# Two experts' tokens sorted at once into transposed form, the usual path behind the test, and one key and value chunk in place of two, in a four-layer model on one core

## The reference, cut to what matters

```python
hid = jax.nn.silu(xi @ w1[e]) * (xi @ w3[e])     # w1, w3: 1024 x 512
return hid @ w2[e]                               # w2: 512 x 1024
...
h = modulate(rms_norm(x, norm_ffn[layer]), sh_f, sc_f)      # hn * (1 + scale) + shift
x = x + gt_f[:, None, :] * hier_moe(h, ...)
```

```python
h = rms_norm_2(x, norm_g) @ w_in
q, kv, gate_logits, z, qm, zm = split_cols_2(h, NSA_IN_SPLITS)
kc, vc, ks, vs, kw, vw = [t.reshape(b, s, g, hd).transpose(0, 2, 1, 3)
                          for t in jnp.split(kv, 6, axis=-1)]
k_cmp = compress_tokens(kc, pe_k, phik_w1, phik_w2)
v_cmp = compress_tokens(vc, pe_v, phiv_w1, phiv_w2)
```

## Time and profile before

| | |
|---|---|
| time, median of 3 (lowest, highest) | 2123.06 us (2120.69, 2127.11) |
| profiled execution: time, span | 2122.02 us, 2120.3 us |
| mean granted TensorE clock | 0.952 of full |
| TensorE matmuls busy | 1914.8 us, 90% of the span |
| VectorE busy | 669.2 us, 32% |
| ScalarE busy | 338.5 us, 16% |
| DMA moved | 588.20 MB, mean 277 GB/s |

### The profile page before, as it was taken

How to read it: one execution, slowest core, us unless ns; L and a number is a source line. 1 busy time by engine, 2 the same in 40 slices (tenths; PEclk the granted TensorE clock), 3 DMA queues, 4 the chain that set the end, 5 groups by cost and what they waited for, 6 DMA issues and landing times.

```text
span 2120.3 us, 27442 instructions
## 1 busy us (share of the span) xinstructions
PE 1914.8 (90%) x11750; PEld 1258.6 (59%) x11750; DVE 669.2 (32%) x1551; ACT 338.5 (16%) x738; POOL 81.0 (4%) x88
## 2 busy tenths in 40 slices
PE   5996669899999999898799999999979998999888
PEld 3745664566555555654466666566558875468754
DVE  2647543222221212671312122112142043301192
ACT  1112112100000000222310000000011123211161
POOL 0000200000000001000000000000100000000000
PEclk8997789999999999999799999999989999999899
DMA  9985505699999999663489999999974343095100
GB/s 353 377 263 192 159 2 238 277 427 427 427 428 428 427 427 414 242 253 124 170 335 423 421 427 428 424 426 426 424 274 159 119 164 109 1 223 170 57 1 30
DMA packets 158880, 588.20 MB, mean 277 GB/s; under 512 B 49612, under 2 KB 57424, under 8 KB 134096
## 3 DMA queue, kind: packets, MB, share of 16 engines
q1 hardware_dynamic: 127024, 560.59, 66.5%
q0 software_dynamic: 8256, 16.63, 2.5%
q10 hardware_dynamic: 23520, 9.86, 1.8%
HBM read 573.50 MB, written 25.23 MB: 282 GB/s over the span
## 4 chain that ended last, share of the span: by engine, by line
PE 68%; DMA 18%; DVE 8%; issue 2%; ACT 2%; PEld 1%; DVEq 1%; ACTq 0%; SPq 0%; PEldq 0%
DMA ring<-in_exp_w_dram 17%; PE bank L712 15%; PE bank L2069 14%; PE bank L2104 6%; PE bank L701 5%; PE bank L843 5%; PE bank L2037 3%; PE bank L2345 3%; PE bank L2335 2%; PE bank L2092 2%; DMA ring<-in_ada_w_dram 1%; PE bank L2045 1%; PE bank L419 1%; DVE pair_probs L3120 1%; DVE pair_probs L3135 1%
## 5 line engine op out<-in xcount | busy, mean ns | idle before, releaser
L2069 PE MATMUL bank<-ring,hidden_room 128*64 128x256 f32 x4096 | 462.2, 381 | 27.6 <-DMA ring<-in_exp_w_dram 24.5
L2069 PEld LDWEIGHTS bank<-ring,hidden_room 128*64 128x64 f32 x4096 | 318.6, 137 | 185.0 <-DMA ring<-in_exp_w_dram 42.1
L712 PE MATMUL bank<-hT,ring 128*128 128x256 f32 x1408 | 311.8, 384 | 5.0 <-ACTq L164 5.0
L712 PEld LDWEIGHTS bank<-hT,ring 128*128 128x128 f32 x1408 | 271.6, 193 | 43.8 <-issue 5.9
L2104 PE MATMUL bank<-ring,hidden_room 128*64 128x512 f32 x1024 | 233.9, 597 | 5.3 <-issue 1.8
L2244 DVE TENSOR_TENSOR hidden_room<-bank,hidden_room 128x256 f32<-128x256 f32 x64 | 27.2, 425 | 471.8 <-ACT hidden_room L2156 471.8
L2104 PEld LDWEIGHTS bank<-ring,hidden_room 128*64 128x64 f32 x1024 | 76.2, 136 | 121.2 <-issue 121.2
L2156 ACT ACTIVATE hidden_room<-bank 128x256 f32<-128x256 f32 x64 | 24.6, 384 | 744.1 <-PE bank L2069 744.1
L2037 PE MATMUL bank<-xn_kept,member 128*64 128x512 f32 x512 | 124.9, 607 | 17.1 <-issue 17.1
L701 PE MATMUL bank<-ring,hT 128*128 128x512 f32 (+2 forms) x288 | 116.0, 564 | 0.0
L1971 POOL DMA_INDIRECT expert_out<-hidden_room,route_spots x60 | 58.6, 977 | 1185.1 <-DVE hidden_room L2258 1171.7
(11 more groups left out here) (583 smaller groups left out, 1835.4 us busy)
## 6 DMA issues: line engine op xcount, KB each, us to landing
ring<-in_exp_w_dram SPq DMA_DIRECT2D x192, 2048.0 KB, 20.6
ring<-in_ada_w_dram SPq DMA_DIRECT2D x24, 2048.0 KB, 21.4
ring<-in_hawk_w_in_dram SPq DMA_DIRECT2D x15, 2048.0 KB, 9.0
ring<-in_even_w_in_dram SPq DMA_DIRECT2D x7, 2048.0 KB
ring<-in_gla_w_in_dram SPq DMA_DIRECT2D x6, 2048.0 KB, 23.3
ring<-in_nsa_w_in_dram SPq DMA_DIRECT2D x5, 2048.0 KB, 7.6
expert_out<-kc POOLq DMA_DIRECT2D x16, 512.0 KB, 12.6
ring<-in_even_w_out_dram SPq DMA_DIRECT2D x2, 2048.0 KB, 7.9
```

Source lines behind the costliest of these rows:

```text
L712: last = nc.tensor.matmul(pair[m // 2][0:rows, (m % 2) * T:(m % 2 + 1) * T], w[:, k, m * P:m * P + rows], src[:, k, :], start=(k == 0), st ...
L2069: last = nc.tensor.matmul(bank[2 + q][halves[half], part * FE // 2:(part + 1) * FE // 2], own[:, q, k % 4, k // 4, :], w[:, k, cols], star ...
```

## The change

Three things change.

1. In the experts' usual path both experts of a pair are sorted at once, 128 columns of `member` as the moving operand and tiles of the tokens as weights, so that the result stands already transposed in the banks 0 and 1: 8 tiles of 2 matmuls. Three tiles stand behind the products L2069 of each expert, one behind the turning of its hidden rows. ScalarE scales and shifts each tile on its way out, eight activations per pair. TensorE waits for the tokens once per pair (and once ahead of the memory products), the turning and VectorE's two passes go, and one comparison per pair makes `member`. The first pair is sorted whole before any product.
2. On TensorE the test is turned round: the usual path stands right behind it, and the path over all tokens behind that.
3. In layer 3 the chunks 2 and 3 become one chunk of 512 columns, each column once. ScalarE evacuates it into half of `pairT`, of `kT` and into a new tile `plain`, and issues four copies between the halves of the partitions, for which VectorE waits before it takes its rows.

```diff
-        cols_of(w, 0, KD, [(1024, 64)] * 2 + [(1088, 64)] * 2 + [(1152, 64)] * 2 + [(1216, 64)] * 2)
-        cols_of(w, 0, KD, [(1280, 64)] * 2 + [(1344, 64)] * 2 + [(1536, 64)] * 2 + [(1600, 64)] * 2)
+        cols_of(w, 0, KD, [(1024, 256), (1280, 128), (1536, 128)])
...
-                        with pe.If(fullest > CAP):
+                        with pe.If(fullest <= CAP):
...
-                            def sort_tokens(e, q):
-                                pe.wait_ge(member_ready.sem, e + 1)
-                                for t in range(TT):
-                                    for half in range(2):
-                                        last = nc.tensor.matmul(bank[0][halves[half], :], member[:, q, t, :],
-                                                                xn[:, t, half * 512:(half + 1) * 512], start=(t == 0), stop=(t == TT - 1))
-                                last.then_inc(sorted_out.sem, 1)
-                            def turn_tokens(e):
...
+                            def sort_tokens(pair, tiles):
+                                if 0 in tiles:
+                                    pe.wait_ge(member_ready.sem, pair + 1)
+                                for k in tiles:
+                                    for t in range(TT):
+                                        last = nc.tensor.matmul(bank[k // 4][:, (k % 4) * P:(k % 4 + 1) * P], xn[:, t, k * P:(k + 1) * P],
+                                                                member[:, t, :, :].rearrange("p q s -> p (q s)"), start=(t == 0), stop=(t == TT - 1))
+                                if KD - 1 in tiles:
+                                    last.then_inc(sorted_out.sem, 1)
...
-                                    pe.wait_ge(own_ready.sem, e + 1)
+                                    if q == 0:
+                                        pe.wait_ge(own_ready.sem, i + 1)
...
-                                    if not closing or q == 0:
-                                        sort_tokens(e + 1, 1 - q)
+                                    if not closing:
+                                        sort_tokens(i + 1, range(4 * q, 4 * q + 3))
...
-                                    if not closing or q == 0:
-                                        turn_tokens(e + 1)
+                                    if not closing:
+                                        sort_tokens(i + 1, range(4 * q + 3, 4 * q + 4))
...
-                            sort_tokens(0, 0)
-                            turn_tokens(0)
+                            sort_tokens(0, range(KD))
                             two_experts(0, 0, True)
                             for a, b in spans(1, PAIRS - 1):
                                 if a in after_pair:
+                                    pe.wait_ge(own_ready.sem, a + 1)
                                     memory_products(pe, a, bank[0], bank[7])
...
-                            def copy_rows(e):
-                                act.wait_ge(sorted_out.sem, e + 1)
-                                nc.scalar.copy(own_rows[:, :], bank[0][:, :]).then_inc(rows_copied.sem, 1)
+                            def own_tokens(pair):
+                                act.wait_ge(sorted_out.sem, pair + 1)
+                                for k in range(KD):
+                                    ins = nc.scalar.activation(own[:, k, :, :].rearrange("p q s -> p (q s)"), bank[k // 4][:, (k % 4) * P:(k % 4 + 1) * P], ACT.Identity,
+                                                               bias=shift[:, k:k + 1], scale=gain[:, k:k + 1])
+                                ins.then_inc(own_ready.sem, 1)
...
+                            def find_members(pair):
+                                shape = [P, TT, 2, CAP]
...
+                            def next_members(pair):
+                                dve.wait_ge(sorted_out.sem, pair)
+                                find_members(pair)
...
+                def to_halves(pair):
+                    first_two, last_two = (pair[b][:, :].rearrange("p (m t) -> p m t", m=2) for b in range(2))
+                    return [(pairT[lower, 0::2, :], first_two[lower], 1.0), (plain[upper], first_two[upper], 1.0),
+                            (pairT[upper, 1::2, 0:T - 1], first_two[upper, :, 1:T], 1.0),
+                            (kT[lower, 0::2, :], last_two[lower], 1.0), (kT[upper, 1::2, :], last_two[upper], 1.0)]
+                def other_halves(act):
+                    act.wait_ge(evacuated_nsa.sem, evacuated_nsa.n)
+                    act.dma_start(pairT[upper, 0::2, 0:T - 1], pairT[lower, 0::2, 1:T]).then_inc(halves_in.up(16), 16)
+                    act.dma_start(pairT[lower, 1::2, :], plain[upper]).then_inc(halves_in.up(16), 16)
+                    act.dma_start(kT[upper, 0::2, :], kT[lower, 0::2, :]).then_inc(halves_in.up(16), 16)
+                    act.dma_start(kT[lower, 1::2, :], kT[upper, 1::2, :]).then_inc(halves_in.up(16), 16)
...
                     dve.wait_ge(evacuated.sem, evacuated.at(3))
+                    dve.wait_ge(halves_in.sem, halves_in.at(64))
```

More of the change, by code:

```diff
@@ L1857, in experts_stage @@
                 y = [[bank[4 + 2 * t + half] for half in range(2)] for t in range(TT)]
-                member = sb(st, "member", [P, 2, TT, CAP])
-                own_rows = room[:, 0:512]
-                own = room[:, 512:1536].rearrange("p (q c h s) -> p q c h s", q=2, c=KD // 2, h=2)
+                member = sb(st, "member", [P, TT, 2, CAP])
+                own = room[:, 512:1536].rearrange("p (k q s) -> p k q s", k=KD, q=2)
                 own_silu = room[:, 1536:2048].rearrange("p (q f) -> p q f", q=2)
@@ L1985, in _ @@
+                        with pe.Else():
                             pe.wait_ge(zeroed.sem, 1)
@@ L2207, in _ @@
                         with dve.Else():
[L2208 to L2224 removed]
+                            def find_members(pair):
+                                shape = [P, TT, 2, CAP]
+                                nc.vector.tensor_tensor(member[:, :, :, :], slots[:, :, bass.ds(2 * pair, 2)].unsqueeze(3).to_broadcast(shape),
+                                                        slot_number.unsqueeze(1).unsqueeze(1).to_broadcast(shape), ALU.is_equal).then_inc(member_ready.sem, 1)
                             def add_rows(t):
@@ L2237, in two_experts @@
                                     if closing and q == 0:
-                                        dve.wait_ge(member_ready.sem, EXPERTS)
+                                        dve.wait_ge(member_ready.sem, PAIRS)
                                         for late_q in range(2):
-                                            ins = nc.vector.tensor_tensor(late[:, late_q], member[:, late_q], late_w[:, :, late_q:late_q + 1].to_broadcast([P, TT, CAP]),
+                                            ins = nc.vector.tensor_tensor(late[:, late_q], member[:, :, late_q, :], late_w[:, :, late_q:late_q + 1].to_broadcast([P, TT, CAP]),
                                                                           ALU.mult)
@@ L2251, in two_experts @@
                                             add_rows(t)
-                                    else:
-                                        own_tokens(e + 1, 1 - q)
                                     dve.wait_ge(y_done.sem, e + 1)
@@ L2926, in nsa_layer @@
                 mq = sb(st, "nsa_mem_q_gate", [P, 4, T])
-                def to_pairs(pair):
-                    copies = []
-                    for b in range(2):
-                        src = pair[b][:, :].rearrange("p (m t) -> p m t", m=2)
-                        copies.append((pairT[0:HD, 2 * b:2 * b + 2, :], src[0:HD], 1.0))
-                        copies.append((pairT[HD:P, 2 * b:2 * b + 2, 0:T - 1], src[HD:P, :, 1:T], 1.0))
-                    return copies
+                lower, upper = slice(0, HD), slice(HD, P)
+                def to_halves(pair):
[9 more added lines that the diff above has]
+                    act.dma_start(kT[lower, 1::2, :], kT[upper, 1::2, :]).then_inc(halves_in.up(16), 16)
                 def memory_query(pair):
```

158 lines of the change are left out of this document (69 added, 89 removed).

## The result

The changed kernel took 2113.81 us in the median of 10 runs (2105.72 to 2120.25), the kernel before 2124.23 (10 runs, 2119.26 to 2129.10). The ratio is 0.9941, with a 95% interval of 0.9925 to 0.9958: 10.4 us between the medians, 12.5 by the ratio. The profiled execution took 2105.72 us (span 2103.9, before 2120.3). So the forecast of 2106 met the profiled execution, which is the fastest of the ten. The median of the executions lies 0.8 us above the end of the range that I gave; the ratio, put on the 2123.06 us from which I forecast, gives 2110.5, inside it. The experiments are about that difference.

What follows compares the result with a forecast made beforehand. Expert stages were taken as bound by fixed-length weight loads from the first release, last-layer projections by TensorE. -13.8 (projection) - 5.5 - 0.5 (starts) + 2.9 (end jumps) = -16.9 us, forecast 2106 us, range 2099 to 2113.

Steps and rivals of the forecast that it cites:

- What bounds the kernel: Expert stages: a fixed-time stream of weight loads from the first freed slots; last layer's projections: TensorE without a break, 107.57 us.
- first release: Expert stages: w1 and w3 slots come free when the first 64 expert products end, at 388.43 and 1069.98 us.
- Projection: Last layer: two chunks of 512 columns become one, 64 of 448 instructions go, copies cost nothing: -13.8 us.
- Inside the stage: Expert pairs: TensorE falls from 27.6 to about 26.7 us against the loads' 30.0, so the sum is 0.
- The starts: Expert stages' starts: sorting begins at the comparison, both experts sorted first; release -0.5 us in layer 0, -5.5 in layer 1.
- The jumps at the end: Expert stages' ends: the usual path's taken branch over the other costs +1.4 us per layer, 2.9 in all, bounds 0 and 8.9.
- cover of 3.6 us: Expert stages' ends: a branch on TensorE is free up to 3.6 us, as VectorE's drain opens the next stage.
- rival 2: Expert stages' ends: jumps cost their upper bound, +6.0 us more, 2112; grounds: layer 1's second gap, full queues; chance 0.12.
- The sum: Whole kernel: -13.8 - 5.5 - 0.5 + 2.9 = -16.9 us against 2122.02, giving 2105.1, so 2106 for the median.
- rival 1: Loop over pairs: 16 instructions longer, its backward branch stops being held; +50 us, 2156; chance 0.03.
- Rival 3: Test before the experts: usual path again behind a jump, so the swap does nothing; -6.2 us, 2117; chance 0.04.
- rival 4: Last layer: copies between halves hold the compression, losing 10 of the 13.8 us; 2116; chance 0.03.

Runs made afterwards that it cites:

- e6: Changed kernel with its closing pair of experts behind the other path, in a second test, so TensorE's far branch comes before the last pair: 2113.48 us, ratio 0.9939.
- e7: As e6, and in addition the first pair's tiles are modulated and handed to TensorE's first products one by one: 2097.86 us, ratio 0.9873.
- e8: As e7, plus 24 unread products of 512 columns behind TensorE's last matmuls of each expert stage: 2145.60 us, ratio 1.0097.
- e9: Changed kernel with the first pair's tiles handed over one by one, far branch left at the stage's end: 2107.16 us, ratio 0.9911.
- e1: Kernel before with the joined projection chunk of layer 3 alone: 2114.26 us, ratio 0.9941.
- e4: Changed kernel without TensorE's path over all tokens, which this input doesn't take, so no far branch: 2103.72 us, ratio 0.9890.
- e5: The changed kernel measured again, nothing altered: 2111.97 us, ratio 0.9939 against the kernel before.
- e2: Kernel before with TensorE's two paths exchanged alone: 2120.81 us, ratio 0.9971.
- e11: As e9, but without TensorE's path over all tokens, so no far branch is left: 2094.89 us, ratio 0.9866.
- e3: Kernel before with the sorting of both experts at once and ScalarE's modulation alone, TensorE's paths in old order: 2125.38 us, ratio 0.9995.
- e10: As e9, with pairs 10 to 15 of the usual path behind the other one, so the far branch comes before pair 10: 2099.75 us, ratio 0.9884.

## Why the prediction was right or wrong

**What bounds the kernel: right.** The stream from the first release to the last w3 block is 449.0 to 450.7 us in layer 0 in all thirteen traces of the table, whatever TensorE did inside; layer 1 gives 460.3 to 461.1 in all but e6, e7 and e8, the three with the branch before the last pair. The first release is the lever: e9 shortened the two starts by 7.5 us in sum against the changed kernel's profile, the stream stayed as long, and the executions gave 7.9.

**Projection: right in mechanism and size.** Forecast -13.8; the chain gives 107.57 - 93.82 = 13.75, and e1 alone -14.7 ± 1.3 at equal clock. The copies are hidden, with 29 us left. My block of 94 us came out at 93.8.

**Inside the stage: the zero was right, a step of it wrong.** I took TensorE's pair to fall from 27.6 to 26.7 us. It is 27.6: the chain has 13.8 us from one block of second products (L2051) at 382.52 to the next at 396.34, as in the earlier trace rows.

```profile
379.24 1.53 PE bank L1989 x12
380.77 1.11 PE bank L2039 x16
381.88 0.64 PE bank L1989 x4
382.52 3.63 PE bank L2051 x16
```

The 32 sortings of a pair take 2 x (1.53 + 0.64) = 4.3 us, not the 3.7 of 0.116 us each, so they save 0.3 of the 4.62 that went, and the rest of the order gives that away. Nothing hangs on it, since the loads' pair is 30.0.

**The starts: direction right, size too large.** Forecast -0.5 and -5.5. In the profiled pair it was 19.35 to 16.97 and 27.78 to 23.14, so -2.4 and -4.6. But I read the old start from a single execution, and e1 showed the same code at 21.4 and 24.9. With two traces of the old start (20.4 and 26.3) and four of the changed one (changed, e4, e5, e6: 18.9 and 22.8) it is -1.4 and -3.5, in sum -4.9 against my -6.0. The clock behind the test is what moves: in e4, e5 and e6 layer 0's first product came 8.5 us after the first sorting, close to the 8.7 of my working, against 6.8 in the changed kernel's profile, whose sorting ran at full clock from its start. That I took each layer "as its own trace went" is the weak step.

**The jumps at the end: direction right, mis-sized.** Forecast +1.4 each by the dearer of the two branches seen. The branch took 5.8 to 6.2 us there in the four traces that have it at the end (changed, e2, e5, e9), and the changed kernel's ends grew by 2.5 and 2.4, in sum +4.9 in place of +2.9. The cover of 3.6 us was right (5.99 - 3.6 = 2.4); the mis-sized term is the branch, 5.9 us for my 5.06. I took both old branches to lie in quiet queues, and that is not what the trace has: the DMA moved 11 GB/s during the one of 3.32 us and 109 during the one of 5.06, and 380 or more during those at the end. So the dearer row was no upper bound for full queues. The growth lies below rival 2's bound. The rule of the Trainium skill ("Runtime: NRT & Kernel Launch", instruction fetch mechanics: a taken branch to a target outside the pages held waits for a DMA) agrees with this: the stall did move with the branch to every place where I put it, and was gone in e4 and e11, where there is no far branch.

**The sum.** With the measured sizes, -13.8 - 4.9 + 4.9 = -13.8, against -12.8 and -14.2 for the changed kernel's two sets. The experts' part is worth nothing on the mean: e1 has the same ratio as the whole, and at equal clock the changed kernel (with e5) is even 2.7 us behind e1, with an uncertainty of 1.4.

That the -16.9 matched the profiled pair (-16.4) was luck, and in two ways. Within the stretches that I touched the pair has -15.9 in place of -13.8, because it has the old start of layer 1 at its longer value and the new one of layer 0 at its shorter. And two stretches that I didn't touch moved as well. Up to the last instruction ahead of layer 0's test it was 369.1 us before and 362.3 after, -6.8. From the first turning behind layer 0's experts to the last instruction ahead of layer 1's test it was 5.1 us more, for the same 784 matmul instructions (before, then changed; the clock is third from the end):

```profile
859.50:1042.20 182.70, 169.03 (x784) 106.86 (x784) 91.57 (x182) 49.91 (x92) 0.00 (x0) 0.93 0.54 201
853.60:1041.40 187.80, 174.27 (x784) 108.80 (x784) 91.55 (x182) 49.83 (x92) 0.00 (x0) 0.89 0.51 190
```

My sum has no term for the clock behind a stage's end.

The parts don't add up either: e2 (-4.6) and e3 (+1.7) together give -2.9, and what the experts' part does behind the projection is +2.7. The starts explain 3.3 us of these 5.6, each by few traces: sorting both experts first costs e2's quick start (17.9 and 20.5) 1.0 and 2.3 us, to the changed kernel's 18.9 and 22.8. The rest is open.

**The rivals.** The loop kept its short backward branch (median 0.208 us, at most 0.244, 28 times), so rival 1 didn't happen. Rival 3 is refuted by the start of the sorting 0.04 us after the comparison, rival 4 by the cover of 29 us. Of rival 2's two grounds the full queues are there, at 4.9 - 2.9 = 2.0 of its 6.0 us; the second gap is not: in the changed kernel the meeting follows the branch within 0.1 us.

**What stays open.** The kernels without a far branch (e4, e11) have a mean clock of 0.9548 against 0.9491 to 0.9528 for all others, worth 6 to 7 us beside the 4.2 to 4.5 that the traces and the equal-clock line show. A part of this is seen in the traces. In all four with the branch at the stage's end (changed, e2, e5, e9) the clock fell 4.8 to 5.4 us ahead of the first turning behind layer 0 and stood at half for 13.7 us; in before, e3, e4, e6, e7 and e11 it fell 2.5 to 3.0 us ahead and stood at half for 6.8; e1, e8 and e10 have 10.2. And the stage from there to layer 1's test goes by its time at half clock: 182.7 to 182.9 us with 24 to 28 us at half in before, e3, e4 and e11; 185.6 to 186.1 with 34 to 35 in e6, e7 and e10; 187.3 to 188.2 with 39 to 40 in the changed kernel, e1, e2, e5, e8 and e9. But e1 is among the longest and has no branch at the end, so the branch alone doesn't decide it, and that TensorE's standing still at the branch is the cause stays argued. Nor do the runs tell why the stretch ahead of layer 0's test, with the same work in all thirteen traces but for the clock, took 362.3 to 372.8 us with 78 to 99 us at half.

## What to carry to other kernels

Exchanging the arms of a test moves the jump's stall to the other end of the usual arm; it gains only what that end can hide better, so look for a place in the middle where the engine waits for loads and has iterations behind it to catch up in (in e10 the stream stayed at 450.1 and 461.0 us). Ahead of a stream of loads, count the whole row of steps up to the first release, and hand over tile by tile there (8 us here, 3 of them in layer 1 by the clock that a pause had cost) before saving instructions inside the stream (0 us here). And where a term rests on a stretch whose clock changes, read it from more than one execution: one pair of profiles gave 16.4 us for a gain of 13.

## What the runs showed of the hardware

- TensorE's far branch took 3.3 to 3.7 us while the DMA moved 11 GB/s (layer 0's start in before, e1, e3), 4.8 to 5.1 us at 109 to 116 GB/s (layer 1's start in the same three), and 5.8 to 6.4 us at 380 to 430 GB/s (all sixteen records within or at the end of the stream of loads). The place in the program differs with the rate, so that the rate is the cause is likely and not shown.
- Behind the far branch before the last pair a second standstill followed within the pair: 2.3 and 2.9 us in layer 1 (e6, e7), 0.7 and 0.9 in layer 0, and in layer 1 of e8 it came after two matmul instructions, for 4.7 us. Behind the branch before pair 10, into a loop (e10), none followed in either layer. Whether the loop is the reason wasn't tried.
- The clock stood at half 4 us after 16 us of unbroken products at full clock (e8); it fell to half in a pause of 2.9 us behind 6.2 us of sorting (changed kernel, layer 1), and stayed at full where the products followed the sorting at once (e7).
- The executions of one kernel spread over 8 to 22 us, and this spread follows the mean granted clock (0.944 to 0.959) by 1.60 us for each 0.001, with 2.0 us of scatter left of about 5.
